# Expert stage with two experts in one row tile, plain fp32 weights and a fixed order of experts

## The reference

```python
g_sel = argmax(softmax(h @ w_rg + b_rg))          # one of 4 groups per token
top_p, top_e = top_k(softmax(le_sel), 2)          # two of its 8 experts
e_idx = g_sel * 8 + top_e                         # 1024 assignments to 32 experts
...
# rows of each expert padded to tiles of 128, one tile at a time:
(silu(xb @ w_e_gate[e]) * (xb @ w_e_up[e])) @ w_e_down[e]
# weighted by w_tok and summed over the two assignments of a token
```

## Time and profile before

| | us |
|---|---|
| median of 3 timed runs | 2765.97 (2765.04 to 2767.08) |
| profiled execution | 2767.67 |
| its span in the trace | 2766.1 |
| PE busy | 2392.0 (86%) |
| DVE busy | 1704.1 (62%) |
| ACT busy | 1206.3 (44%) |
| POOL busy | 156.6 (6%) |
| mean granted PE clock | 0.914 |
| DMA, mean over the span | 144 GB/s |

### The profile page before, as it was taken

How to read it: one execution, slowest core, us unless ns; L and a number is a source line. 1 busy time by engine, 2 the same in 40 slices (tenths; PEclk the granted TensorE clock), 3 DMA queues, 4 the chain that set the end, 5 groups by cost and what they waited for, 6 DMA issues and landing times.

```text
span 2766.1 us, 30016 instructions
## 1 busy us (share of the span) xinstructions
PE 2392.0 (86%) x10748; PEld 1872.6 (68%) x10748; DVE 1704.1 (62%) x2115; ACT 1206.3 (44%) x1589; POOL 156.6 (6%) x158
## 2 busy tenths in 40 slices
PE   4989858955999999995798958999999976999997
PEld 2778533444777777774576857788877765788775
DVE  6777633134888888885565454577753464577742
ACT  3222411025888888884435615432333243432332
POOL 0000000001211221220000200000000000000000
PEclk8989978967999999998899959999999967999999
DMA  7513200119999999983021000222322300223221
GB/s 309 228 61 105 78 0 31 61 34 357 354 358 350 372 360 362 358 342 138 31 92 61 31 1 32 92 91 91 108 101 95 122 1 4 88 95 112 97 91 61
DMA packets 38448, 397.95 MB, mean 144 GB/s; under 512 B 8800, under 2 KB 9184, under 8 KB 15456
## 3 DMA queue, kind: packets, MB, share of 16 engines
q1 hardware_dynamic: 27520, 374.75, 35.7%
q0 software_dynamic: 10848, 22.08, 2.2%
HBM read 388.40 MB, written 21.02 MB: 148 GB/s over the span
## 4 chain that ended last, share of the span: by engine, by line
PE 56%; DVE 11%; ACT 5%; issue 3%; DMA 1%; ACTq 0%; DVEq 0%; POOL 0%; SPq 0%; POOLq 0%
PE PS L496 10%; PE PS L498 10%; PE PS L497 10%; PE PS L653 6%; PE PS L655 6%; PE PS L654 6%; DVE A L1506 2%; DVE ring_r L1725 2%; PE PS L478 1%; ACT w_hi_r L1145 1%; PE PS L619 1%; DVE hid_r L1948 1%; PE PS L936 1%; DVE ring_r L1694 1%; PE PS L768 1%
## 5 line engine op out<-in xcount | busy, mean ns | idle before, releaser
L1725 DVE TENSOR_TENSOR ring_r<-ring,w_hi_r 128x1024 fp32r<-128x1024 f32 x196 | 238.6, 1223 | 361.9 <-ACT w_hi_r L1145 361.9
L496 PE MATMUL PS<-h_hi_r,w_hi_r 128*128 128x512 f32 x1056 | 418.4, 396 | 18.2 <-DVE h_r L1733 10.6
L497 PE MATMUL PS<-h_r,w_hi_r 128*128 128x512 f32 x1104 | 432.4, 392 | 0.0
L498 PE MATMUL PS<-h_hi_r,ring_r 128*128 128x512 f32 x1056 | 413.5, 392 | 0.0
L653 PE MATMUL PS<-h_r,top_r 128*128 128x512 f32 x768 | 315.0, 410 | 34.7 <-DVE ring_r L1694 34.7
L1145 ACT ACTIVATE w_hi_r<-ring 128x1024 fp32r<-128x1024 f32 x196 | 202.2, 1050 | 317.6 <-PE PS L498 197.8
L1118 ACT ACTIVATE h_r<-A 128x1024 fp32r<-128x1024 f32 x256 | 266.2, 1059 | 49.4 <-PE PS L655 49.4
L496 PEld LDWEIGHTS PS<-h_hi_r,w_hi_r 128*128 128x128 f32 x1056 | 199.8, 189 | 70.4 <-issue 17.3
L497 PEld LDWEIGHTS PS<-h_r,w_hi_r 128*128 128x128 f32 x1104 | 209.3, 190 | 45.3 <-issue 1.9
L498 PEld LDWEIGHTS PS<-h_hi_r,ring_r 128*128 128x128 f32 x1056 | 199.6, 189 | 41.9
L1694 DVE TENSOR_TENSOR hid_r<-A,h_r 128x1024 fp32r<-128x1024 f32 x176 | 208.0, 1220 | 24.4 <-ACT h_r L1118 22.6
(11 more groups left out here) (406 smaller groups left out, 4338.2 us busy)
## 6 DMA issues: line engine op xcount, KB each, us to landing
A<-wexp SPq DMA_DIRECT2D x64, 2048.0 KB, 8.8
ring<-wall SPq DMA_DIRECT2D x63, 2048.0 KB, 8.2
ring<-wexp SPq DMA_DIRECT2D x32, 2048.0 KB, 8.8
A<-wada SPq DMA_DIRECT2D x12, 2048.0 KB, 12.1
x<-xt_in SPq DMA_DIRECT2D x2, 2048.0 KB, 14.0
A<-y_assignments SPq DMA_DIRECT2D x4, 1024.0 KB, 8.0
h_tokens<-A SPq DMA_DIRECT2D x4, 512.0 KB, 2.8
A<-att_bias SPq DMA_DIRECT2D x1, 2048.0 KB, 12.6
```

The source lines that it names most:

```text
L496: mm(out, w[0], x_[0], start=first, stop=False)
L497: mm(out, w[0], x_[1], start=False, stop=False)
L498: return mm(out, w[1], x_[0], start=False, stop=last_)
L1725: tt(ring_r[:, slot, :, cols], ring[:, slot, :, cols], w_hi_r[:, :, cols].bitcast(F32), ALU.subtract).then_inc(S("w_lo"), 1)
```

## The change

Two experts now share one pass in another way, and the order of experts is fixed: pair `i` is experts `2i` and `2i + 1`, 16 pairs, then extra pairs only for an expert with more than 96 rows (`CAP`), as many as needed; an expert's first 64 rows go into half of a 128-row tile (`x_main`), the next 32 into a quarter of a second tile (`x_rest`, 64 rows for both experts). DVE's slot arithmetic and constants follow that. A pair gathers 128 + 64 rows.

PE multiplies plain fp32 weights, not split ones. In the main products the stationary operand is 128x64, one expert's rows, and the outputs go to the two halves of a bank; in the rest products it is 128x32 and four products, gate and up of both experts, go to the four quarters of bank 5. A pair has five products (`m_pc` counts them): gate main, up main, rest, down main, down rest. The next pair's rows are turned between the third and the fourth.

Eight weight tiles are held: gate twice for both experts (`moe_gate[q]`), up and down once for both. The loads of pair 0, the gates and later the ups and downs of pair 1 have fixed addresses and stand before SP's reading of the loop count; the first three are issued after `m_out`, further ones after `merged`, `w_out0`, `w_out1` and the logits. The loop runs over double passes `d` (pairs `q` = 0 and 1). ACT and DVE no longer split anything in the loop.

```diff
-NB = 2 * T // P + E
+HALF, QUARTER = 64, 32
+CAP = HALF + QUARTER
+PAIR_ROWS = 2 * CAP
+PAIRS = E // 2
+MORE = 2 * T // (CAP + 1)
+PAIRS_ALL = PAIRS + MORE
+SLOT_COLS = -(-(PAIRS_ALL + 1) * PAIR_ROWS // P)
...
+        moe_up, moe_dn = [A[:, 0:8], A[:, 32:40]], [A[:, 24:32], h[:]]
+        moe_gate = [[A[:, 8:16], A[:, 16:24]], [ring[:, 0], ring[:, 1]]]
+        xg = [A[:, 40:42, :], A[0:HALF, 42:44, :]]
+        x_main, x_rest = A[:, 44:46, :], A[:, 46, :]
+        hid_main, hid_rest = A[:, 47, :], A[0:HALF, 48, :]
+        hT_main, hT_rest = A[:, 49, :], A[:, 50, 0:4 * HALF]
+        yb = [A[:, 51:53, :], A[0:HALF, 53:55, :]]
+        DOUBLES_MIN, DOUBLES_MAX = PAIRS // 2, -(-PAIRS_ALL // 2)
...
+            def gate_of(q, j, e):
+                sp.dma_start(moe_gate[q][j], e[:, 0].rearrange("a p k n -> p (a k) n")).then_inc(S(f"wg{q}{j}"), 16)
+            def up_of(j, e):
+                sp.dma_start(moe_up[j], e[:, 1].rearrange("a p k n -> p (a k) n")).then_inc(S(f"wu{j}"), 16)
+            def down_of(j, e):
+                sp.dma_start(moe_dn[j], e[:, 2].rearrange("a p k n -> p (a k) n")).then_inc(S(f"wd{j}"), 16)
+            sp.wait_ge(S("mm"), TILE_DONE[G_MOUT + 1][3])
+            gate_of(0, 0, wexp[0:1])
+            gate_of(0, 1, wexp[1:2])
+            up_of(0, wexp[0:1])
+            sp.wait_ge(S("merged"), KD)
+            up_of(1, wexp[1:2])
+            sp.wait_ge(S("mm"), UNIT_USED["w_out0"])
+            gate_of(1, 0, wexp[2:3])
+            sp.wait_ge(S("mm"), UNIT_USED["w_out1"])
+            down_of(0, wexp[0:1])
+            gate_of(1, 1, wexp[3:4])
             for t in range(NT):
                 sp.wait_ge(S("ht_ev"), t + 1)
-                sp.dma_start(f_tok[t * P:(t + 1) * P, :], A[:, 2 * t:2 * t + 2, :].rearrange("p a b -> p (a b)")).then_inc(S("f_tok"), 16)
-            n = pairs(sp)
-            sp.wait_ge(S("f_tok"), 16 * NT)
-            def expert(b, j, part):
-                e = sp.value_load(blki[0:1, bass.ds(b, 1)], min_val=0, max_val=E - 1)
-                return wexp[bass.ds(e, 1), part].rearrange("a p k n -> p (a k) n")
-            order = [(0, 0), (0, 1), (1, 0), (1, 1), (0, 2), (1, 2)]
-            for j, part in [(0, 0), (0, 1), (0, 2), (1, 0), (1, 1), (1, 2)]:
-                if (j, part) == (1, 0):
-                    sp.wait_ge(S("xg0"), 16)
-                sp.dma_start(moe_w[j][part], expert(j, j, part)).then_inc(S(f"w{j}{part}"), 16)
-            with sp.Fori(1, n) as i:
-                for j, part in order:
-                    rwait(sp, S("m_pc"), m_used(i, 19 + 4 * j if part == 2 else 8 * j + 4 * part + 3, back=1))
-                    sp.dma_start(moe_w[j][part], expert(2 * i + j, j, part)).then_inc(S(f"w{j}{part}"), 16)
+                sp.dma_start(f_tok[t * P:(t + 1) * P, :], A[:, 40 + 2 * t:42 + 2 * t, :].rearrange("p a b -> p (a b)")).then_inc(S("f_tok"), 16)
+            sp.wait_ge(S("logits"), 1)
+            down_of(1, wexp[1:2])
...
             for j in range(2):
+                sp.wait_ge(S("m_pc"), m_done(0, 2))
+                up_of(j, wexp[2 + j:3 + j])
+            for j in range(2):
+                sp.wait_ge(S("m_pc"), m_done(0, 4))
+                down_of(j, wexp[2 + j:3 + j])
+            n = doubles(sp)
+            def expert(i, j):
+                e = sp.value_load(blki[0:1, bass.ds(2 * i + j, 1)], min_val=0, max_val=E - 1)
+                return wexp[bass.ds(e, 1)]
+            with sp.Fori(1, n) as d:
+                for q in range(2):
+                    es = [expert(2 * d + q, j) for j in range(2)]
+                    rwait(sp, S("m_pc"), 2 * PRODUCTS * d + m_done(q - 2, 2))
+                    for j in range(2):
+                        gate_of(q, j, es[j])
+                    rwait(sp, S("m_pc"), 2 * PRODUCTS * d + m_done(q - 1, 2))
+                    for j in range(2):
+                        up_of(j, es[j])
+                    rwait(sp, S("m_pc"), 2 * PRODUCTS * d + m_done(q - 1, 4))
+                    for j in range(2):
+                        down_of(j, es[j])
...
+            def rows_T(count):
+                for j in range(2):
+                    pe.wait_ge(S(f"xg{j}"), count)
                 for k in range(KD):
+                    last = nc.tensor.transpose(PS[:, k // 4, (k % 4) * P:(k % 4 + 1) * P], xg[0][:, k // 4, (k % 4) * P:(k % 4 + 1) * P], ident)
                 last.then_inc(S("m_tr"), 1)
+                for k in range(KD):
+                    last = nc.tensor.transpose(PS[:, 2, k * HALF:(k + 1) * HALF], xg[1][:, k // 4, (k % 4) * P:(k % 4 + 1) * P], ident[0:HALF, 0:HALF])
                 last.then_inc(S("m_tr"), 1)
 
+            def main_of(bank, w):
+                for k in range(KD):
+                    for j in range(2):
+                        last = mm(PS[HALF * j:HALF * (j + 1), bank, :], x_main[:, k // 4, (k % 4) * P + HALF * j:(k % 4) * P + HALF * (j + 1)],
+                                  w[j][:, k, :], start=k == 0, stop=k == KD - 1)
+                last.then_inc(S("m_pc"), 1)
+            rows_T(16)
+            with pe.Fori(0, n) as d:
+                for q in range(2):
+                    for j in range(2):
+                        pe.wait_ge(S(f"wg{q}{j}"), 16 * d + 16)
+                    pe.wait_ge(S("m_x"), 4 * d + (2 * q + 1))
+                    main_of(3, moe_gate[q])
+                    for j in range(2):
+                        pe.wait_ge(S(f"wu{j}"), 32 * d + 16 * (q + 1))
+                    main_of(4, moe_up)
+                    pe.wait_ge(S("m_x"), 4 * d + (2 * q + 2))
+                    pe.wait_ge(S("m_y1"), 2 * d + (q + 1))
+                    for k in range(KD):
+                        for part, w in enumerate((moe_gate[q], moe_up)):
+                            for j in range(2):
+                                r = HALF * part + QUARTER * j
+                                last = mm(PS[r:r + QUARTER, 5, :], x_rest[:, k * HALF + QUARTER * j:k * HALF + QUARTER * (j + 1)], w[j][:, k, :],
+                                          start=k == 0, stop=k == KD - 1)
                     last.then_inc(S("m_pc"), 1)
+                    pe.wait_ge(S("m_h"), 4 * d + (2 * q + 1))
+                    for k in range(4):
+                        last = nc.tensor.transpose(PS[:, 3, k * P:(k + 1) * P], hid_main[:, k * P:(k + 1) * P], ident)
+                    last.then_inc(S("m_tr"), 1)
+                    rows_T(32 * d + 16 * (q + 2))
+                    pe.wait_ge(S("m_h"), 4 * d + (2 * q + 2))
+                    for k in range(4):
+                        last = nc.tensor.transpose(PS[:, 4, k * P:(k + 1) * P], A[:, 48, k * P:(k + 1) * P], ident)
+                    last.then_inc(S("m_tr"), 1)
+                    pe.wait_ge(S("m_ht"), 2 * d + (q + 1))
+                    pe.wait_ge(S("m_y0"), 2 * d + (q + 1))
+                    for j in range(2):
+                        pe.wait_ge(S(f"wd{j}"), 32 * d + 16 * (q + 1))
+                    for half in range(2):
+                        for k in range(4):
+                            for j in range(2):
+                                last = mm(PS[HALF * j:HALF * (j + 1), 6 + half, :], hT_main[:, k * P + HALF * j:k * P + HALF * (j + 1)],
+                                          moe_dn[j][:, 4 * half + k, :], start=k == 0, stop=k == 3)
+                    last.then_inc(S("m_pc"), 1)
+                    pe.wait_ge(S("m_hr"), 2 * d + (q + 1))
+                    for k in range(4):
+                        for half in range(2):
+                            for j in range(2):
+                                r = HALF * half + QUARTER * j
+                                last = mm(PS[r:r + QUARTER, 5, :], hT_rest[:, k * HALF + QUARTER * j:k * HALF + QUARTER * (j + 1)],
+                                          moe_dn[j][:, 4 * half + k, :], start=k == 0, stop=k == 3)
+                    last.then_inc(S("m_pc"), 1)
 
...
+            def rows_out(count):
                 act.wait_ge(S("m_tr"), count)
+                a_(x_main, PS[:, 0:2, :], ACT.Copy).then_inc(S("m_x"), 1)
+                act.wait_ge(S("m_tr"), count + 1)
+                a_(x_rest, PS[:, 2, :], ACT.Copy).then_inc(S("m_x"), 1)
+            rows_out(1)
+            with act.Fori(0, n) as d:
+                for q in range(2):
+                    done, turned = 2 * PRODUCTS * d, 8 * d
+                    act.wait_ge(S("m_pc"), done + m_done(q, 0))
+                    a_(hid_main, PS[:, 3, :], ACT.Silu).then_inc(S("m_sg"), 1)
+                    act.wait_ge(S("m_pc"), done + m_done(q, 2))
+                    a_(hid_rest, PS[0:HALF, 5, :], ACT.Silu).then_inc(S("m_sg"), 1)
+                    act.wait_ge(S("m_tr"), turned + (4 * q + 3))
+                    a_(hT_main, PS[:, 3, :], ACT.Copy).then_inc(S("m_ht"), 1)
+                    rows_out(turned + (4 * q + 4))
+                    act.wait_ge(S("m_pc"), done + m_done(q, 3))
+                    rwait(act, S("sc0"), 32 * d + 16 * (q + NT))
```

(84 more changed lines are left out.)

175 lines of the change are left out of this document (44 added, 131 removed).

## The result

The changed kernel took 2914.4 us (median; 2911.9 to 2921.8) against 2766.0 for the one before: a ratio of 1.054 [1.053, 1.055], 148 us more where 29 less were forecast, and outside the range. Its profiled execution spans 2911.8 us.

The account below looks back on a forecast made before the run. PE with its weight splits was taken to lead, DMA close behind. 16 pairs at 37.4 us plus 2.2 slow start less 2.8 make the loop 597.8 (-20.0); with the start -28.8, so 2737 us, range 2684 to 2790.

Parts of the forecast that it names:

- What bounds the kernel: Expert stage of the old kernel: PE with its weight splits leads, DMA follows closely, 38.5 us a pass.
- the bytes: Expert stage: both kernels read 96 weight tiles; DMA needs 33 to 36 us a pair with gathers and scatters.
- PE's new work: Expert loop: main and rest products, transposes and handovers take PE alone 33.8 us a pair, against 38.5.
- the second rival: Rest products: four-way tiles run two at a time, +10.35 us, period 44.2, 2849 us; chance 0.10 including a small part for weight loading.
- open weight loads: PE's products: by a skill rule, loads would not overlap matmuls, some 10 us a pair; left out of the sum.
- Weights in time: SP's loop loads: all weights have 6 us or more to spare, unless DMA becomes the period at 38.
- Token rows: the new wait: PE's transposes of the next pair's gathered rows: rows land at 24.0, wait 2.8 us, ends 0 and 9.7.
- The clock: PE after a pause: lower clock costs 1.7 us, in half of the pairs, so 0.8 a pair.
- Start: Before the expert loop: early weight loads leave an idle queue, first product 8.8 us earlier, at 643.6.
- The sum: Whole kernel: loop 597.8 against 617.8 us, -20.0; with the start -28.8, giving 2737.
- No row wait: Rival, expert loop: gathers land by 21.2, period 33.8 to 35.5, 2682 to 2710 us; chance 0.17.
- Rows or DMA later: Rival, expert loop: slower index loads and landing or DMA, period above 38.9, no change to +60 us; chance 0.18.

## Why the prediction was wrong, step by step

**What bounds the kernel, the bytes, splits.** Held. DMA was put at 33 to 36 us a pair; with the rows in time it carries six tiles and the rows in 34.2, at 400 GB/s.

**PE's new work.** Held: 33.8 us a pair forecast, 34.2 measured wherever nothing is late. The four 32-column tiles do run at once, so the second rival (2849, tiles by twos) is out; that its time is nearer to the result than mine is chance. The 10 us a pair of open weight loads are out too: 32 records with a load before each take 7.0 us, 0.22 each.

**Weights in time.** Held: no wait for one in the change, nor in the kernels that reach 34.2 with all weights.

**Token rows: the new wait.** This is the step that failed. Its mechanism was right and its size was not: 2.8 us forecast with an upper end of 9.7, and 13.5 measured. Link by link, from the first product of a pair:

| | forecast | measured (pair at 775.15) | no weights queued |
|---|---|---|---|
| first index load issued | 4.5 | 4.3 | 4.4 |
| first gather | 11.0 | 12.4 | 7.3 |
| second index load | 13.0 | 14.4 | 9.3 |
| second gather | 17.3 | 25.1 | 12.6 |
| its rows landed | 24.0 | about 34.6 | about 16.8 |

The first link took the 6.5 us that the earlier trace rows has at its longest, and got 8.1. The second took 4.3, between the two rows, and got 10.7 (789.58 to 800.28): it was priced as if the four tiles had been through by then, though at the prediction's own 5.0 to 5.5 us a tile they fill the engines for over 20 us, and the up tiles follow. The landing took the loop's median of before less a share for 64 rows, 6.7, and got 9.5 here. Together 1.4 + 6.4 + 2.8 = 10.6 of the 10.7 missing.

The upper end of 9.7 was no bound either, but not because the old trace had nothing longer. The earlier trace rows is one pass. All of L2063 in the kernel before reads:

```profile
DMA to landing us min/median/max: 2.0/5.5/10.1
```

Its loads alternate, mostly 2 to 3 us for the first of a pass and 6 for the second; in three passes the second took 9.1, 9.9 and 10.1, the last of them (1091.29 to 1102.19) a link of 10.9. With 10.9 for the second link and the longest landing, 11.4, the prediction's own sum would have ended at 11.0 + 2.0 + 10.9 + 11.4 = 35.3, which takes in the 34.6 measured. What was rare before became the rule when SP began to ask for four tiles at once, where it had been held tile for tile. Why the second index load, with half the rows, takes longer than the first (landing in 9.7 to 10.1 us against 6.5 to 7.6, 700 to 1200 us) isn't shown by any run.

**The clock.** 0.8 us a pair were allowed, for half of the pairs. Every pair with a wait pays, and 2.5 us (the run with PE kept busy), 3.0 by difference: 50.7 - 34.2 - 13.5. After a pause of 13 us PE works some 8 us at 0.50, where 3.4 us were read off.

**Start.** 8.8 earlier forecast, 15.8 measured, of which 2.9 aren't the change's: the burst of the earlier trace rows at 503.53 begins at 500.67 here, with the same work before it (501.3 to 503.0 in other runs of this kernel's experiments). From there to POOL's first scatter it is 0.5 longer (forecast +0.4), its eight scatters take 0.3 less, and then, against the earlier trace rows: last scatter to index load 2.7 us for 10.1 (-7.4, forecast -5.4), index load to first gather 2.9 for 6.1 (-3.2, forecast -2.4), the second gather 1.3 behind it (forecast +1.0), from the gather that ends last to turned rows 6.6 for 6.8 (-0.2, forecast +0.9), then to the product 1.1 for 4.7 (-3.6, forecast -3.3). The links are those of the forecast; the idle queue gave more than was taken.

**The sum.** Fourteen pairs at 50.7 for 37.4 are +186, the first and last pair and the slow start -4, the start -7: +175 of the 177 us between forecast and result.

**The rivals.** "No row wait" had 2682 to 2710; the kernels with the table in SBUF are just that, at 2685.6 and 2690.8. "Rows or DMA later" was what happened, and it had 0.18, but its size was off as well, at most +60 us where +148 came: its worst case, 30.9 + 12.6 = 43.5 a pair, took 6.5 for each index load and left out the clock. With the links as measured and 3 for the clock it comes to 34.6 + 12.6 + 3 = 50.

## What to carry to other kernels

Price a chain of small dependent transfers at the queue that the new kernel makes around it, and take the longest landing from all instances in the old trace, not from one pass: an 8-byte-a-row load that lands in 2.2 us alone took 8.7 beside four queued weight tiles, and two of them stand in series in each pair, between a scatter and a gather. Take the serial loads out of the loop, and issue the gathers before anything that they needn't wait for; their own slowness then costs nothing. When an engine is made faster so that its loads are asked for in bursts, look first for who shares the DMA engines with them.

## What was not expected of the hardware

- Four 32-column tiles run at once in fp32 at the full rate. The group of the rest products of gate and up (busy us, mean ns of one, idle before) has 113.1 us over 16 pairs, 7.07 each. 64 records run in that time, 0.110 each, where one alone takes 0.431; 48 of them a pair on average are in this group, the others beside them read `ring`. The earlier trace rows had shown two tiles only. The Trainium skill ("TensorEngine Tiling (Array Packing)", Theoretical Speedup) allows up to 4x, and this trace agrees.

```profile
L664 PE MATMUL PS<-A 128*32 128x512 f32 x768 | 113.1, 594 | 0.0
```

- A gather of 64 rows under load lands little sooner than one of 128 rows, with half the bytes: 9.3 to 10.5 us against 10.7 to 11.7 in the changed kernel, 700 to 1200 us.
- DMA kept 400 GB/s at a share of 1.00 for 300 us with small gathers and scatters among the weights, above the 380 that the prediction took as its mean.
